# One rounded product of 256 columns for a token's gate map in the second lookup, its two halves added behind PSUM

## The reference, cut to what matters

```
def peer(h, w_q, sub_keys, u, v):
    T, D = h.shape
    q = (h @ w_q).reshape(T, PEER_HEADS, 2, PEER_QDIM // 2)
    s = jnp.einsum('thpd,hpnd->thpn', q, sub_keys)
    sv, si = lax.top_k(s, PEER_TOPK)
    cand = (sv[:, :, 0, :, None] + sv[:, :, 1, None, :]).reshape(T, PEER_HEADS, 256)
    fv, fi = lax.top_k(cand, PEER_TOPK)
    ...
    idx = (i1 * PEER_NKEYS + i2).reshape(T, PEER_HEADS * PEER_TOPK)
    g = jax.nn.softmax(fv, axis=-1).reshape(T, PEER_HEADS * PEER_TOPK)
    act = gelu(einsum('td,ted->te', h, u[idx]))
    out = einsum('te,ted->td', g * act, v[idx])
```

## Time and profile before

| | |
|---|---|
| median of 3 runs | 4292.49 us (4286.0 to 4293.88) |
| profiled execution, span | 4284.8 us |
| TensorE busy | 98% |
| VectorE busy | 72% |
| ScalarE busy | 42% |
| GpSimd busy | 31% |
| mean granted TensorE clock | 0.992 |

### The profile page before, as it was taken

The page is one execution under the profiler, slowest core; times in us unless marked ns, Lnnn a source line. Parts: engine busy times, 40 slices in busy tenths (PEclk is TensorE's granted clock), DMA queues, the critical chain, the costliest instruction groups (busy, mean ns, idle before and its releaser), DMA issues.

```text
span 4284.8 us, 61360 instructions
## 1 busy us (share of the span) xinstructions
PE 4186.1 (98%) x24253; PEld 3726.7 (87%) x24253; DVE 3070.5 (72%) x4932; ACT 1794.5 (42%) x2979; POOL 1331.5 (31%) x699
## 2 busy tenths in 40 slices
PE   8999999999999999999999999999999999999999
PEld 5888778888888799867999999999999799998887
DVE  5775557877887676465589798788887675554676
ACT  3233352233233544264244776333334645444444
POOL 0000200000000100000378666777772058444443
PEclk9999999999999999999999999999999999999999
DMA  6543215544555365212477899999994156778885
GB/s 273 224 166 144 87 40 206 220 180 188 220 200 199 113 247 191 79 40 70 145 242 254 291 345 348 367 363 353 357 355 164 60 199 220 226 245 285 282 286 181
DMA packets 286591, 926.87 MB, mean 216 GB/s; under 512 B 19680, under 2 KB 170336, under 8 KB 212192
## 3 DMA queue, kind: packets, MB, share of 16 engines
q1 hardware_dynamic: 249440, 788.70, 51.7%
q0 software_dynamic: 36864, 134.23, 8.7%
HBM read 837.92 MB, written 84.93 MB: 215 GB/s over the span
## 4 chain that ended last, share of the span: by engine, by line
PE 87%; DVE 5%; DMA 3%; ACT 2%; POOL 1%; issue 1%; SPq 0%; ACTq 0%; POOLq 0%; DVEq 0%
PE bank L1136 25%; PE bank L1137 25%; PE bank L1138 25%; PE bank L1574 3%; PE bank L1329 1%; PE bank L1131 1%; PE bank L1126 1%; PE bank L1122 1%; PE bank L1341 1%; POOL weight_ring_low L2964 1%; PE bank L1366 1%; DMA gates<-work 1%; DVE work L2701 1%; DVE weight_ring_low L2282 1%; ACT work L1884 0%
## 5 line engine op out<-in xcount | busy, mean ns | idle before, releaser
L2964 POOL TENSOR_TENSOR weight_ring_low<-weight_ring,up_high 128x1024 fp32r<-128x1024 f32 x233 | 587.6, 2527 | 1065.0 <-ACT up_high L2030 1063.4
L1138 PE MATMUL bank<-peer_h_high,weight_ring_low 128*128 128x256 f32 (+2 forms) x2240 | 699.0, 312 | 0.0
L1136 PE MATMUL bank<-peer_h_high,up_high 128*128 128x384 f32 (+1 forms) x2048 | 643.7, 314 | 13.7 <-POOL weight_ring_low L2964 9.2
L1137 PE MATMUL bank<-h_low,up_high 128*128 128x384 f32 (+1 forms) x2048 | 634.5, 310 | 0.0
L2117 ACT ACTIVATE down_high<-weight_ring 128x1024 fp32r<-128x1024 f32 x256 | 257.0, 1052 | 525.9 <-PE bank L1138 525.9
L1138 PE MATMUL bank<-h_high,weight_ring_low 128*128 128x512 f32 (+1 forms) x1280 | 464.2, 363 | 0.0
L1136 PE MATMUL bank<-h_high,in_high 128*128 128x512 f32 (+1 forms) x1216 | 441.4, 363 | 0.3
L1137 PE MATMUL bank<-h_low,in_high 128*128 128x512 f32 (+1 forms) x1216 | 441.0, 363 | 0.0
L2928 POOL TENSOR_SCALAR h<-work,params 128x256 f32<-128x256 f32 x12 | 11.8, 997 | 1377.9 <-PE bank L1481 874.8
L1138 PEld LDWEIGHTS bank<-peer_h_high,weight_ring_low 128*128 128x128 f32 x2240 | 426.8, 191 | 3.8
L2728 DVE TENSOR_TENSOR weight_ring_low<-weight_ring,down_high 128x1024 fp32r<-128x1024 f32 x128 | 310.6, 2427 | 161.8 <-ACT down_high L2117 161.8
(11 more groups left out here) (424 smaller groups left out, 10081.1 us busy)
## 6 DMA issues: line engine op xcount, KB each, us to landing
weight_ring<-in_up SPq DMA_DIRECT2D x128, 1024.0 KB, 5.5
weight_ring<-in_down SPq DMA_DIRECT2D x128, 1024.0 KB, 6.3
weight_ring<-in_mod_w SPq DMA_DIRECT2D x112, 1024.0 KB, 5.0
weight_ring<-in_ffn_in SPq DMA_DIRECT2D x88, 1024.0 KB, 6.9
weight_ring<-in_ffn_out SPq DMA_DIRECT2D x64, 704.0 KB, 5.3
gates<-work SPq DMA_DIRECT2D x40, 1024.0 KB, 9.8
gelu<-work SPq DMA_DIRECT2D x64, 384.0 KB, 6.8
work<-gates SPq DMA_DIRECT2D x32, 768.0 KB, 12.6
```

What stands on the lines that cost most here:

```text
L1136: mm(dst, w_high, a_high, start=first, stop=False)
L1137: mm(dst, w_high, a_low, start=False, stop=False)
L1138: return mm(dst, w_low, a_high, start=False, stop=last)
L2964: G.tensor_tensor(ring_low[:, slot, w], ring[:, slot, w], up_high[:, n % 3, :].bitcast(F32), ALU.subtract)\
```

## The change

In layer 1 the two matrices of marks are now in the rounded form (fp32r) that the up units use. The gate is split into a rounded part `gate_high` and the rest `gate_low` (`split_gates`, once). A token's first marks are two 128-column halves side by side in the free upper columns of `peer_h_high` and `h_low`: marks times `gate_high` in the left half, made by ScalarE (`weigh_marks`, eight instructions a turn, as in layer 0), and marks times `gate_low` in the right half, made in place by VectorE (`low_marks`). A token's map is one rounded product of 256 columns; the eight tokens of a turn fill all four PSUM banks. ScalarE copies the left halves to the tile (`begin_gates`, four instructions of 256 elements), VectorE adds the right halves from PSUM (`join_gates`, four instructions of 256) and signals `gates_copied`, on which TensorE waits before the next turn's maps. VectorE's order in a turn is marks(q + 1), join_gates(q), split in even q, low_marks(q + 1); ScalarE's is gelus and roundings, weigh_marks(q + 1), begin_gates(q). Layer 0 is unchanged.

```diff
--- before.py
+++ after.py
@@ -498,7 +498,8 @@
         sub_squared, sub_rooted, sub_scaled = sem("sub_squared"), sem("sub_rooted"), sem("sub_scaled")
         keys_scored, keys_read, picks_ready = sem("keys_scored"), sem("keys_read"), sem("picks_ready")
         softmax_in, softmax_out, routed_copied = sem("softmax_in"), sem("softmax_out"), sem("routed_copied")
-        marks_ready, marks_weighted = sem("marks_ready"), sem("marks_weighted")
+        marks_ready, marks_weighted, marks_high = sem("marks_ready"), sem("marks_weighted"), sem("marks_high")
+        gates_begun = sem("gates_begun")
         gates_done, gates_copied = sem("gates_done"), sem("gates_copied")
         gates_stored = [sem(f"gates_stored{b}") for b in range(2)]
         gates_loaded = [sem(f"gates_loaded{b}") for b in range(2)]
@@ -688,9 +689,21 @@
 
         take = scratch()
         first_mark, second_mark = take(2, SUB, P), take(2, SUB, P)
+        mark_rows = high_low("mark_rows", [P, 2, SUB, P], work_at, 2 * SUB * P)
+        gate_high = high_low("gate_high", [P, TL], work_at)[:, :]
+        gate_low = work[:, TL:2 * TL]
+
+        mark_pairs = [part[:, :, TL:T].rearrange("p t (a k) -> p t a k", a=2) for part in (peer_h_high, h_low)]
+        assert SUB == KC and TL == 2 * P
         gate_tiles = {1: take(2, NKEYS, BLOCK)}
         at8 = lambda n: work[:, HP * T:HP * T + n]
         gate_tiles[0] = at8(2 * NKEYS * BLOCK).rearrange("p (a b c) -> p a b c", a=2, b=NKEYS)
+
+        def half_gates(q, e):
+
+            k0 = q % 2 * SUB + 2 * e
+            parts = ps[KEY_BANK + e][:, :].rearrange("p (t a k) -> p a k t", a=2, k=P)
+            return gate_tiles[1][:, q // 2 % 2, :, k0:k0 + 2], (parts[:, 0], parts[:, 1])
 
         take = scratch()
         gate_rest = take(2, T // BLOCK, GROUP, BLOCK)
@@ -1566,6 +1579,14 @@
 
                     b = q // 2
                     pe.wait_ge(marks_weighted, 2 * g0 + q + 1)
+                    if l == 1:
+                        for c in range(2):
+                            wait_for(pe, gates_copied, 4 * g0 + 2 * (q - 1) + c + 1)
+                            for k in range(4 * c, 4 * c + 4):
+                                i = mm(ps[KEY_BANK + k // 2][:, k % 2 * TL:k % 2 * TL + TL], mark_rows[:, q % 2, k],
+                                       mark_pairs[q % 2][:, k].rearrange("p a k -> p (a k)"), start=True, stop=True)
+                            i.then_inc(gates_done, 1)
+                        return
                     for c in range(2):
                         bank = KEY_BANK + 2 * (q % 2) + c
 
@@ -2053,6 +2074,17 @@
                         A(gate_tile[:, b % 2, :, 4 * c:4 * c + 4], ps[KEY_BANK + c][:, :].rearrange("p (t k) -> p k t", k=P),
                           ACT.Copy).then_inc(gates_copied, 1)
 
+                def begin_gates(q):
+
+                    if q % 2 == 0:
+                        wait_for(act, gates_stored[q // 2 % 2], 16 * (g0 // 2 + q // 4))
+                    for c in range(2):
+                        act.wait_ge(gates_done, 4 * g0 + 2 * q + c + 1)
+                        for e in range(2):
+                            dst, (high, low) = half_gates(q, 2 * c + e)
+                            i = A(dst, high, ACT.Copy)
+                        i.then_inc(gates_begun, 1)
+
                 for k in range(3, 8):
                     round_unit(name, s, k)
                 for n in range(3):
@@ -2060,6 +2092,13 @@
                 def weigh_marks(q):
 
                     act.wait_ge(marks_ready, 2 * g0 + q + 1)
+                    if l == 1:
+                        for k in range(SUB):
+                            token = q * SUB + k
+                            pair = mark_pairs[q % 2][:, k]
+                            i = A(pair[:, 0], pair[:, 1].bitcast(F32), ACT.Copy, scale=gate_high[:, token:token + 1].bitcast(F32))
+                        i.then_inc(marks_high, 1)
+                        return
                     for k in range(SUB):
                         token = q * SUB + k
                         i = A(first_mark[:, q % 2, k, :], first_mark[:, q % 2, k, :], ACT.Copy, scale=routed[:, 2, token:token + 1])
@@ -2092,13 +2131,16 @@
                       ACT.Copy).then_inc(routed_copied, 1)
                 for b in range(blocks):
                     for q in range(2 * b, 2 * b + 2):
-                        if l == 0 and q == 0:
+                        if q == 0:
                             weigh_marks(0)
                         for n in half_of(gates[b], q % 2):
                             gelu(n)
-                        if l == 0 and q + 1 < 2 * blocks:
+                        if q + 1 < 2 * blocks:
                             weigh_marks(q + 1)
-                        copy_gates(q)
+                        if l == 0:
+                            copy_gates(q)
+                        else:
+                            begin_gates(q)
                 for n in rest[:-2]:
                     gelu(n)
                 if l == 0:
@@ -2812,13 +2854,29 @@
                     wait_for(dve, gates_done, 4 * g0 + 2 * (q - 1))
                     tokens = slice(q * SUB, q * SUB + SUB)
                     every = spread(turn_iota, 1, SUB)
-                    V.tensor_tensor(second_mark[:, q % 2], every, spread(routed[:, 1, tokens], 2, P), ALU.is_equal)
-                    first = first_mark[:, q % 2]
+                    V.tensor_tensor((second_mark if l == 0 else mark_rows)[:, q % 2], every, spread(routed[:, 1, tokens], 2, P), ALU.is_equal)
+                    first = first_mark[:, q % 2] if l == 0 else mark_pairs[q % 2][:, :, 1]
                     V.tensor_tensor(first, every, spread(routed[:, 0, tokens], 2, P), ALU.is_equal).then_inc(marks_ready, 1)
-                    if l == 0:
-                        return
-                    dve.wait_ge(marks_ready, 2 * g0 + q + 1)
-                    V.tensor_tensor(first, first, spread(routed[:, 2, tokens], 2, P), ALU.mult).then_inc(marks_weighted, 1)
+
+                def split_gates():
+
+                    link(V.tensor_copy(gate_high, routed[:, 2, LAT]))
+                    link(subtract(gate_low, routed[:, 2, LAT], gate_high))
+
+                def low_marks(q):
+
+                    dve.wait_ge(marks_high, q + 1)
+                    low = mark_pairs[q % 2][:, :, 1]
+                    V.tensor_tensor(low, low.bitcast(F32), spread(gate_low[:, q * SUB:q * SUB + SUB], 2, P), ALU.mult).then_inc(marks_weighted, 1)
+
+                def join_gates(q):
+
+                    for c in range(2):
+                        dve.wait_ge(gates_begun, 2 * q + c + 1)
+                        for e in range(2):
+                            dst, (high, low) = half_gates(q, 2 * c + e)
+                            o = V.tensor_tensor(dst, dst, low, ALU.add)
+                        o.then_inc(gates_copied, 1)
 
                 def split_up(n):
 
@@ -2827,12 +2885,20 @@
                     dve.wait_ge(up_rounded, e0 + n + 1)
                     subtract(ring_low[:, slot, w], ring[:, slot, w], up_high[:, n % 3, :]).then_inc(up_split_dve, 1)
 
+                if l == 1:
+                    split_gates()
                 marks(0)
+                if l == 1:
+                    low_marks(0)
                 for q in range(2 * blocks):
                     if q + 1 < 2 * blocks:
                         marks(q + 1)
-                    if l == 1 and q % 2 == 0:
-                        split_up(split_beside(l)[q // 2])
+                    if l == 1:
+                        join_gates(q)
+                        if q % 2 == 0:
+                            split_up(split_beside(l)[q // 2])
+                        if q + 1 < 2 * blocks:
+                            low_marks(q + 1)
                     if l == 0:
                         for c in range(1 + q % 2):
                             picked_product(picked_at["half", q, c])
```

## The result

The changed kernel takes 4371.4 us (median of four runs, 4370.2 to 4375.0) against 4292.2 for the kernel before; the ratio is 1.0185, with a 95% interval of 1.0173 to 1.0197. Forecast were 4366 us, range 4335 to 4405.

The account below looks back on a forecast made before the run. TensorE bounds the stretch before; after, a VectorE-ScalarE ring does. Sixteen turns of 11.58 and 15 of 7.96 us, with a later start, add 73 us to the 4284.8 us span: 4358, plus 7.7 to the median, 4366 us; range 4335 to 4405.

Parts of the forecast that it names:

- The stretch belongs to TensorE, and its gain would be 26 us: Layer 1's gate maps: TensorE alone sets the pace; the new product saves 0.82 us a turn, 26 us in all.
- By shares all fits; the order decides: Per turn VectorE needs 4.8 or 6.0 us, ScalarE 5.9, below TensorE's 6.72; program order on both engines decides.
- The ring of 7.96 us: Loop over VectorE and ScalarE, one low_marks to the next: marks, scalings, copies, adds; 7.96 us without a split.
- GpSimd gets its turn between split and low_marks: In turns with a split, GpSimd's waiting subtract goes ahead of low_marks and adds 2.40 us: 9.18 becomes 11.58.
- a block 19.54 us: Two turns of the map stretch, one with VectorE's split and GpSimd's turn, one without, last 19.54 us.
- TensorE's side has 1.64 us to spare: From split to scaling, TensorE's unit, gelu and rounding take 4.31 us against VectorE's 5.95, so TensorE isn't last.
- the slow clock costs 0: TensorE idles some 4 us a block; half clock for 6.8 us would cost 1.24 a block, +20; taken as 0.
- The turns of 11.58 and 7.96 us: Map stretch: 16 turns of 11.58 us with a split and 15 of 7.96 without, 304.7 us.
- The signs: Expected in the map window: TensorE about 70% busy, maps alternately 11.6 and 8.0 us apart, low_marks 3 us or more every second turn.
- the second rival: GpSimd doesn't get ahead of low_marks; TensorE's side is last, two turns 17.96 us, 4339 us; chance 0.17.
- The start: Ahead of the maps: split_gates meets GpSimd's subtract; first map at 3658.9 us, before at 3654.0.
- What follows the last map: Eight up units, store and load of the maps: taken as unchanged, 0 to 1.3 us.

Follow-up runs that it names:

- e6: Changed kernel without low_marks and join_gates, so the output leaves out the gates' low part; 4269.4 us.
- e10: Changed kernel with ScalarE's copies ahead of the next turn's scalings, all layer 1 up-unit splits on GpSimd, gates split behind the first marks; 4266.9 us.
- e3: Changed kernel with one swap on ScalarE: copies of turn q ahead of the scalings of turn q + 1; 4292.1 us.
- e2: Changed kernel with VectorE's split of an up unit moved from behind the adds to ahead of the marks of the same turn; 4321.6 us.
- e7: Changed kernel with all layer 1 splits of up units on GpSimd, none on VectorE; 4304.7 us.
- e5: Changed kernel with 15 unread TensorE products ahead of each wait for VectorE's split, filling TensorE's gap; 4366.7 us.
- e1: Changed kernel with gate_low kept in a free part of PSUM bank 7, so low_marks has one SBUF operand only; 4372.1 us.
- e9: Changed kernel with both gate_low in PSUM and 15 unread TensorE products ahead of each wait for VectorE's split; 4341.7 us.

## Why the prediction was right, and where it wasn't

- *The stretch belongs to TensorE, and its gain would be 26 us.* Right: e6 and e10 have it, 26 us in the stretch.
- *By shares all fits; the order decides.* Right, and the main step: e3 and e2 reorder the same instructions and move the time by 79 and 50 us.
- *The ring of 7.96 us.* Right to 0.1 us (e7, 7.88). Each size was that of a row: scalings 2.44 (2.34 to the next start), adds 1.42, copies 1.17. By the Trainium skill's table (VectorE: DVE Perf Modes, section The TRN2 errata) four copies are, as an estimate, 1.43 us; the trace says 1.17, and the trace decides.
- *GpSimd gets its turn between split and low_marks.* Right as an event: 3.40 us in 15 of 16 blocks of the changed kernel, 3.42 in e5. In the first block low_marks starts 0.26 us ahead of GpSimd's subtract; there it takes 1.22 us and the subtract 3.22. The Trainium skill (SBUF — State Buffer, section SBUF: two separate sides) leaves open who is next; here it is the one that waited first. Wrong as to what it is worth: I had it as what makes a block 19.54 us, and e1 shows that without it the block is the same.
- *TensorE's side has 1.64 us to spare, the slow clock costs 0.* This is the step that failed. I bounded the clock at 0 to 20 us and took 0. A gap of 3.8 us came in 15 of 16 blocks, and at each the granted clock fell to half, for 3.4 or 6.8 us. The unit then took 5.5 us to its gelu, and TensorE's side, not VectorE's, was last in all 15 blocks that a scaling follows. By my own bound a fall of 6.8 us costs 1.24 us a block; nine blocks show 1.0 to 1.3. Cost: 10.7 us of the stretch (e5 against the changed kernel).
- *The turns of 11.58 and 7.96 us.* My sum for the stretch was high by 6 us the other way (305.7 against e5's 299.5): a turn with the split was 11.21 us in e5, since split and GpSimd's turn together add 3.33 us to the ring where I had 1.22 + 2.40. Together the stretch was 310.2 us against 305.7 forecast, and 4371 us against 4366: the small miss is partly luck, two errors that cancel.
- *The signs.* Of those that I named, low_marks above 3 us in every second turn came true, and the map matmuls are 0.12 us apart at full clock. TensorE's share came out at 81% where I had about 70%: the window's 1090 records at 0.12 us would be 69%, and those behind the gaps ran at half clock. The maps were 12.1 to 13.2 and 7.1 us apart, not 11.6 and 8.0; the 7.1 is the short turn of the second rival, in which TensorE's side is last. So the number was the forecast's and the path was nearer to the rival's, with the slow clock on it.
- *The start.* 4.9 us forecast, 4.7 measured; the conversion did wait for GpSimd (2.23 us in place of 0.28, the latter in e10).
- *What follows the last map.* Taken as unchanged; 392.0 against 393.4 us. The one fall of the granted clock there lasted 3.4 us in place of 6.8 (by my estimate 1.7 us less), so the 0 to 1.3 us that I allowed here can be neither seen nor ruled out.
- *The span of before as the base.* The profiled execution was the fastest of its runs, and 9.5 us of the two spans' difference lie ahead of the stretch; using the median kept this out of the forecast.

## What to carry to other kernels

When work is moved between two engines that hand it back and forth, add up the ring, from an instruction to the same one a turn later, along each engine's program order; shares of 60% busy on every engine don't bound it. What ends last on the path must be taken away together with what lies beside it: measure the two causes in all four combinations before calling one of them worthless. And before a change of this kind is dropped, exchange two calls: here that turned 79 us lost into none, and with the splits given to GpSimd and the gates split later too (e10), into 22 us gained.

## What the runs showed of the hardware that I had not expected

At each of 15 gaps of TensorE of 3.8 us, one in some 20 us, the granted clock fell to 0.50 for 3.4 or 6.8 us, which made 0.87 over the window; with the gap filled by products nobody reads it was 1.00. e9's blocks, with that filling in them, last 17.9 us, as the forecast's sum had them without it (17.96), so the filling cost nothing that shows. GpSimd's waiting subtract came ahead of a VectorE instruction that was ready and stood directly behind another on its engine, in 15 of 16 blocks, with no idle time between the two.
